# Rotary halves exchanged by transfers, and four stick-breaking steps placed ahead of the last value unit

## The reference

```python
def partial_rope(x, cos, sin):            # ROPE_DIM = 16 of 64 features of a head
    xr = x[..., :ROPE_DIM].astype(jnp.float32)
    x1, x2 = xr[..., :ROPE_DIM // 2], xr[..., ROPE_DIM // 2:]
    rot = jnp.concatenate([x1 * cos - x2 * sin, x2 * cos + x1 * sin], axis=-1)
    return jnp.concatenate([rot.astype(x.dtype), x[..., ROPE_DIM:]], axis=-1)
...
        z = jnp.einsum("bhtd,bhsd->bhts", qb, kb) * scale
        log_not = jnp.where(causal, jax.nn.log_sigmoid(-z), 0.0)
        tail = lax.cumsum(log_not, axis=3, reverse=True) - log_not
        log_a = jax.nn.log_sigmoid(z) + tail
        a = jnp.where(causal, jnp.exp(log_a), 0.0)
        outs.append(jnp.einsum("bhts,bhsd->bhtd", a, vb))
```

## Time and profile before

| | us |
|---|---|
| median of 3 runs | 2310.27 |
| profiled execution | 2309.9 |
| its span | 2307.8 |
| mean granted TensorE clock | 0.986 of full |

### The profile page before, as it was taken

The page is one execution under the profiler, slowest core; times in us unless marked ns, Lnnn a source line. Parts: engine busy times, 40 slices in busy tenths (PEclk is TensorE's granted clock), DMA queues, the critical chain, the costliest instruction groups (busy, mean ns, idle before and its releaser), DMA issues.

```text
span 2307.8 us, 28179 instructions
## 1 busy us (share of the span) xinstructions
PE 2234.9 (97%) x10366; PEld 1771.7 (77%) x10366; DVE 944.0 (41%) x1289; ACT 823.8 (36%) x1362; POOL 974.6 (42%) x435
## 2 busy tenths in 40 slices
PE   8999999999998999999999999999999889999997
PEld 6888887875556788888777888888877568888886
DVE  3211346356874411234675311134552653111345
ACT  4222335324873322223532422223342654222222
POOL 4444444553003544444443454444443434544442
PEclk9999999999998999999999999999999899999999
DMA  5222232432001322323232232222222002322221
GB/s 188 91 95 105 91 111 89 127 110 74 1 1 55 110 91 91 104 97 109 73 110 73 82 118 91 101 100 91 91 91 75 17 1 92 109 100 100 91 93 70
DMA packets 29799, 202.66 MB, mean 88 GB/s; under 512 B 3360, under 2 KB 4000, under 8 KB 6048
## 3 DMA queue, kind: packets, MB, share of 16 engines
q1 hardware_dynamic: 28800, 198.55, 24.5%
q10 hardware_dynamic: 928, 3.14, 0.4%
HBM read 198.54 MB, written 2.10 MB: 87 GB/s over the span
## 4 chain that ended last, share of the span: by engine, by line
PE 69%; DVE 4%; ACT 1%; issue 1%; POOL 1%; DVEq 0%; ACTq 0%; POOLq 0%
PE PS L946 20%; PE PS L948 20%; PE PS L947 20%; PE PS L1377 1%; PE PS L1238 1%; PE PS L1197 1%; PE PS L1269 1%; DVE NMAX L1667 1%; PE PS L1361 1%; PE PS L1389 1%; DVE ACC L1434 1%; PE PS L1017 0%; POOL X L479 0%; PE PS L1220 0%; DVE TMP L1514 0%
## 5 line engine op out<-in xcount | busy, mean ns | idle before, releaser
L454 POOL TENSOR_TENSOR WL<-RAW,WH 128x1024 fp32r<-128x1024 f32 x368 | 908.5, 2473 | 1234.4 <-ACT WH L521 1234.4
L946 PE MATMUL PS<-XH,WH 128*128 128x512 f32 (+1 forms) x2200 | 865.9, 394 | 28.9 <-DVE XL L1426 19.8
L948 PE MATMUL PS<-XH,WL 128*128 128x512 f32 (+1 forms) x2200 | 853.2, 388 | 0.0
L947 PE MATMUL PS<-XL,WH 128*128 128x512 f32 (+1 forms) x2200 | 852.8, 388 | 0.0
L521 ACT ACTIVATE WH<-RAW 128x1024 fp32r<-128x1024 f32 x368 | 388.1, 1059 | 1255.4 <-PE PS L948 1211.2
L946 PEld LDWEIGHTS PS<-XH,WH 128*128 128x128 f32 x2200 | 415.4, 189 | 125.1 <-issue 27.6
L947 PEld LDWEIGHTS PS<-XL,WH 128*128 128x128 f32 x2200 | 415.7, 189 | 86.6 <-issue 4.1
L948 PEld LDWEIGHTS PS<-XH,WL 128*128 128x128 f32 x2200 | 415.3, 189 | 84.8
L946 PE MATMUL PS<-HH,WH 128*128 128x512 f32 x672 | 261.4, 389 | 0.0
L947 PE MATMUL PS<-HL,WH 128*128 128x512 f32 x672 | 261.4, 389 | 0.0
L948 PE MATMUL PS<-HH,WL 128*128 128x512 f32 x672 | 261.4, 389 | 0.0
(11 more groups left out here) (194 smaller groups left out, 1558.2 us busy)
## 6 DMA issues: line engine op xcount, KB each, us to landing
RAW<-wstream SPq DMA_DIRECT2D x183, 1024.0 KB, 4.8
X<-xT SPq DMA_DIRECT2D x4, 512.0 KB, 9.0
WORK<-memT ACTq DMA_DIRECT2D x2, 1024.0 KB, 5.4
outT<-WORK SPq DMA_DIRECT2D x8, 256.0 KB, 2.1
RAW<-wstream SPq DMA_DIRECT2D x2, 512.0 KB, 6.3
PB<-WORK ACTq DMA_DIRECT2D x8, 127.8 KB, 2.3
CST<-consts SPq DMA_DIRECT2D x1, 912.0 KB, 10.6
WORK<-constsb SPq DMA_DIRECT2D x1, 256.0 KB, 12.4
```

Source lines behind the costliest of these rows:

```text
L454: pool.tensor_tensor(WL[:, s, :, :].rearrange("p a b -> p (a b)"), RAW[:, s, :], WH[:, s, :, :].rearrange("p a b -> p (a b)").bitcast(F), ...
L946: pe.matmul(o, wh, xh, start=start, stop=False)
L947: pe.matmul(o, wh, xl, start=False, stop=False)
L948: return pe.matmul(o, wl, xh, start=False, stop=stop)
```

## The change

Three things, the third in support of the second.

First, PERM and the matmul with it go. ScalarE, after it has rounded the next weights in a rotary job, waits for the take of that same job and issues four transfers of 8 partitions x 512 values within SBUF, from SQ to LT, which exchange the two halves of each rotary group; the other rows of LT are set to zero once at the start. The sign is in SIN. `rope` waits for the four transfers and reads LT where it read PSUM. TensorE's first attention scores wait for the takes of proj1 where `flip` did.

Second, `SB_AHEAD = 4`: steps 0 to 3 of stick-breaking are issued by TensorE before unit sv 5, and by VectorE and ScalarE before their wait for that unit. The last value units use banks 2, 3, 6, 7, two of them are transposed into their own banks, and the transposes of sv 5 go behind tails 0 and 1 and pair 4/5. The last kv unit releases the chunks of XH one by one (`XH_USERS` gains "kv").

Third, GpSimd splits units 2 and 3 of outB after the low parts of steps 0 to 7, not before them.

```diff
+def flip_bank(x):
+    return x["bank"] if x["kind"] == "sv" and x["j"] >= 4 else 4 + x["f"] % 2
...
-            split_units(first, U0["outB"] + RING)
-            low_softplus()
+            split_units(first, U0["outB"] + 2)
+            low_softplus(0, 8)
+            split_units(U0["outB"] + 2, U0["outB"] + RING)
+            low_softplus(8, len(SBSTEPS))
...
+            def rotate(x):
+                act.wait_ge(taken, x["t"] + 1)
+                for a in (0, DH):
+                    for b in (0, 8):
+                        act.dma_start(LT[a + b:a + b + 8, x["c"] % 2, :],
+                                      SQ[a + 8 - b:a + 16 - b, x["f"] % 2, :]).then_inc(rotated[x["c"] % 2], 16)
...
+                    if part == "kv" and n == len(jobs) - 1:
+                        turn(jobs[n - 2])
+                        for t in range(SB_AHEAD):
+                            sb_exp_ln(t)
                     unit(x["u"])
...
+                    if x["kind"] in ROTARY:
+                        rotate(x)
                     if x["kind"] == "vs":
                         round_b(0)
                     if x["kind"] == "ks" or (x["kind"], x["j"]) == ("nq", 1):
                         raw_hidden()
...
-                if x["kind"] in ROTARY:
-                    mm = pe.matmul(PS[:, 4 + f % 2, :], PERM, SQ[:, f % 2, :], start=True, stop=True)
...
+                        if part == "kv" and i == len(jobs) - 1:
+                            pe.wait_ge(taken, jobs[i - 2]["t"] + 1)
+                            for t in range(0, SB_AHEAD, 2):
+                                sb_pair(t)
                         features(x["u"], x["bank"], stage, first=x["n"] == 0,
...
+            for t in range(SB_AHEAD, n + LAG_V, 2):
+                if SB_AHEAD < t < n:
+                    sb_pair(t)
                 if 0 <= t - LAG_T < n:
                     sb_tail(t - LAG_T)
                     sb_tail(t + 1 - LAG_T)
+                if t == SB_AHEAD:
+                    sb_pair(t)
+                    flip(JOBS["kv"][-1])
+                if t == LAG_V:
+                    pe.wait_ge(turned, FLIPS[max(FLIPS)]["c"])
...
-                dve.wait_ge(flipped, f + 1)
-                chain(dve.tensor_tensor(TMP[:, 1, :], SIN, PS[:, 4 + f % 2, :], ALU.mult))
+                dve.wait_ge(rotated[x["c"] % 2], 64 * ((x["c"] + 1) // 2))
+                chain(dve.tensor_tensor(TMP[:, 1, :], SIN, LT[:, x["c"] % 2, :], ALU.mult))
...
+                    if last and part == "kv":
+                        for t in range(SB_AHEAD):
+                            sb_step(t)
...
+            chain(dve.memset(LT[:, :, :], 0.0))
```

More of the change, by code:

```diff
@@ L106, in bank_of @@
         return dict(slot=slot, bank=n % 4, free=t - 3 if n >= 4 else 0, after=False)
+    if part == "kv" and slot >= 16:
+        return dict(slot=slot, bank=slot - (14 if slot < 18 else 12), free=0, after=True)
     if slot >= 18:
@@ L142 @@
 FLIPS = {x["f"]: x for v in JOBS.values() for x in v if "f" in x}
+for _f, _x in FLIPS.items():
+    _x["clear"] = max([FLIPS[g]["c"] for g in range(_f % 2, _f, 2) if FLIPS[g]["kind"] in TURNED], default=0)
 XN = {n: i for i, n in enumerate(
@@ L232 @@
 LAG_T = 4
+SB_AHEAD = 4
 LAG_V = 6
@@ L354, in program @@
         flipped = sem("flipped")
+        rotated = [sem(f"rotated{i}") for i in range(2)]
         turned = sem("turned")
@@ L811, in project @@
                     round_unit(x["u"] + RING)
-                    if n >= 2 and jobs[n - 2]["kind"] in TURNED:
+                    if n >= 2 and jobs[n - 2]["kind"] in TURNED and not (part == "kv" and n == len(jobs) - 1):
                         turn(jobs[n - 2])
@@ L923, in sb_weights @@
                 act.activation(ASLOT[t % 4][:, 0:w], PS[:, t % SBANKS, 0:w], ACT.Exp).then_inc(sb_a, 1)
-            for t in range(n + LAG_T):
+            for t in range(SB_AHEAD, n + LAG_T):
                 if t >= LAG_T:
@@ L1126, in hidden_turned, with sb_scores, sb_strict, sb_tail @@
                 mm.then_inc(hid_turned, 1)
+            def sb_scores(t):
+                h, j = SBSTEPS[t]
+                if t == SB_AHEAD:
+                    pe.wait_ge(turned, FLIPS[max(FLIPS) - 2]["c"])
+                if t >= SBANKS:
+                    pe.wait_ge(sb_a, (t | 1) - SBANKS + 1)
+                r = slice(DH * (h % 2), DH * (h % 2) + DH)
+                pe.matmul(PS[:, t % SBANKS, 0:S - j * P], W[r, 8 + h // 2, j * P:(j + 1) * P],
+                          Q[r, h // 2, j * P:S], start=True, stop=False, skip_group_check=True)
+            def sb_strict(t):
+                pe.matmul(PS[:, t % SBANKS, 0:P], IDB, CSB[:, B_STRICT:B_STRICT + P], start=False, stop=False,
+                          skip_group_check=True).then_inc(sb_qk, 1)
+            def sb_tail(t):
+                h, j = SBSTEPS[t]
+                w = S - j * P
+                pe.wait_ge(sb_lo, t + 1)
+                bank = PS[:, t % SBANKS, :]
+                for n in range(NT - j):
+                    col, width, m = n * P, w - n * P, SUMS[:, 1 if n == 0 else 0, :]
+                    for part in (XH, XL):
+                        mm = pe.matmul(bank[:, col:w], m, part[:, (t - 2 * n) % 8, sb_cols(t - 2 * n, width)], start=False,
+                                       stop=n == NT - j - 1 and part is XL, skip_group_check=True)
+                mm.then_inc(sb_tri, 1)
+            def sb_values(t):
+                h, j = SBSTEPS[t]
+                c = h // 2
+                w = S - j * P
+                pe.wait_ge(sb_a, t + 1)
+                if h % 2 == 0 and j == NT - 1 and c >= 2:
+                    pe.wait_ge(sb_o, c - 1)
+                r = slice(DH * (h % 2), DH * (h % 2) + DH)
+                pe.matmul(PS[r, 6 + c % 2, j * P:S], V_SB[:, j, h * DH:(h + 1) * DH], ASLOT[t % 4][:, 0:w],
+                          start=j == NT - 1, stop=j == 0, skip_group_check=True).then_inc(sb_pv, 1)
+            def sb_pair(t):
+                sb_scores(t)
+                sb_scores(t + 1)
+                sb_strict(t)
+                sb_strict(t + 1)
             def project(part, stage, norm=None):
@@ L1154, in project @@
                         ssq(norm, 7)
-                    if i >= 1 and "f" in jobs[i - 1]:
+                    if i >= 1 and jobs[i - 1]["kind"] in TURNED:
                         flip(jobs[i - 1])
@@ L1163, in project @@
                         mem_step(MEM_BESIDE[part], k)
-                if "f" in jobs[-1]:
+                if jobs[-1]["kind"] in TURNED and part != "kv":
                     flip(jobs[-1])
@@ L1170, in scores @@
                     pe.wait_ge(roped, 10)
+                    pe.wait_ge(taken, TAKEN["proj1"] - 1)
+                if part == "mix1" and y["s"] == 2:
+                    pe.wait_ge(taken, TAKEN["proj1"])
                 if y["p"] == 4 * 4:
@@ L1350, in _ @@
             project("kv", "kv")
-            pe.wait_ge(taken, TAKEN["kv"])
-            pe.wait_ge(turned, FLIPS[max(FLIPS)]["c"])
+            pe.wait_ge(sums_ready, 1)
             n = len(SBSTEPS)
[L1356 to L1376, removed]
-                        mm = pe.matmul(bank[:, col:w], m, part[:, (t - 2 * n) % 8, sb_cols(t - 2 * n, width)], start=False,
-                                       stop=n == NT - j - 1 and part is XL, skip_group_check=True)
-                mm.then_inc(sb_tri, 1)
```

150 lines of the change are left out of this document (66 added, 84 removed).

## The result

The changed kernel took 2324.18 us (median of 5 runs, 2321.47 to 2326.82), against 2311.05 us for the kernel before on the same chip: ratio 1.006, 95% interval 1.0048 to 1.0073. One of the five runs of the kernel before took 6142.08 us, for a reason that nothing here shows, and the ratio leaves it out. Forecast were 2299.3 us and a range from 2294.5 to 2308. The profiled execution has a span of 2322.3 us, 14.5 us more than before.

The account below looks back on a forecast made before the run. The prediction took TensorE, busy 97% of the span, as the bound. Its terms, - 10.2 + 0.3 + 0.7 - 2.3 + 0.5 = - 11.0 us, gave 2299.3 us, range 2294.5 to 2308.

Parts of the forecast that it names:

- Part 1: In proj1, rotary swap matmuls leave PE's unbroken run: 12 x 0.85 = 10.2 us saved.
- Part 2: In proj1, ACT's transfers and L1556 reading LT replace the swap: small lag, 0.3 us wait ahead of w1v 0.
- the one called the weakest: On ACT's queue in rotary jobs, each 8-row transfer within SBUF was taken to cost 0.33 to 0.4 us to issue.
- The second step: In dk 0 to dk 3, DVE's lag was to grow by 0.05 us a job at 0.33 us an issue.
- Rival B: In proj1, 0.6 us issues or 6.2 us landings make PE stand 9 us twice: + 7.0, 2317 us; chance 0.12.
- Part 3: At the start of attention, L1556 waits for POOL's split and L1557 follows: first maxima + 0.7 us.
- Part 4: Around the last value unit, four steps ahead: pair 6/7 - 2.3 us, POOL's later outB splits + 0.5 us.
- Rival C: In the 512-wide scores, PE's granted clock changes: 2295.0 us (chance 0.10) or 2302.2 us (chance 0.08).
- the two of the loop: In proj1's rotary jobs: issues at 0.33 to 0.4 us, and lag growing 0.05 us a job at 0.33 us.

Follow-up runs that it names:

- the run with late ropes: The changed kernel, but VectorE ropes a job behind the next take also where a small w1 unit stands between; 2297.33 us, ratio 0.9956.

## Why the prediction was wrong

**Part 1, right.** The price of the swaps is best read in the run with late ropes, where PE waits only 0.2 us. From dk 0's take to nq 3's, in DVE's timelines, first before, then with late ropes:

```profile
453.74 0.69 DVE L1631 TENSOR_TENSOR SQ<-RSTD,PS 128x512 f32<-128x512 f32 x1 [5.24 <-PE PS L948]
...
547.92 0.69 DVE L1628 SCALAR_TENSOR_TENSOR SQ<-PS,RSTD 128x512 f32<-128x512 f32 x1 [2.71 <-PE PS L948]
```
```profile
453.26 0.69 DVE L1717 TENSOR_TENSOR SQ<-RSTD,PS 128x512 f32<-128x512 f32 x1 [5.25 <-PE PS L970]
...
537.21 0.69 DVE L1714 SCALAR_TENSOR_TENSOR SQ<-PS,RSTD 128x512 f32<-128x512 f32 x1 [1.11 <-PE PS L970]
```

94.18 less 83.95 is 10.2 us. That is net of the wait ahead of w1v 0, forecast at 0.3 us and measured there at 0.2, so the 12 swaps were 10.4 us (in the changed kernel itself that wait is gone, the stand before it having covered it).

**Part 2, wrong, in two steps of it.** The first is the one called the weakest: an issue at 0.33 to 0.4 us. It is 0.63. L819, of the same kind and engine, was the row to go by, and the reasons for setting it aside (odd row length, more rows) were guesses: 8 and 16 rows cost the same. The Trainium skill, "DMA: Bandwidth & Descriptors", on issuing engines that are not separate queues, calls the time to initiate a transfer "usually small relative to the DMA itself". For four small transfers in a row it isn't, by this trace: the issues take 2.6 us, and the last lands 2.7 us after its own began (481.41) or 2.0 us (in the dq run).

The second step would have taken most of the gain by itself: with four issues at 0.32 us the stretch from dk 0's take to the first maxima gained 2.5 us and not 9.2. The forecast let the lag grow by 0.05 us a job at 0.33 us, because it kept ACT's first rounding and POOL's first split at their places in PE's time and let only the second of each move with the take. But ACT's wait for `taken` stands ahead of both, so a take that is late enough moves both roundings, the two splits behind them, and the rope that must wait for the splits. From the rows above, closed, the period is 0.7 (take) + 4d (issues) + 0.1 + 1.1 (first rounding) + 5.2 (two splits) + 0.5 (rest of the rope) = 7.6 + 4d: 10.1 us at d = 0.63 (measured 10.2). With two issues of 0.63 it gives 8.9 (measured 8.9), with two of 0.60, 8.8 (measured 8.8), and with four of 0.32, 8.9 (measured 9.0 in every second job and 6.7 in the others). What the forecast called a lag of tenths tips into this regime as soon as both roundings are caught.

Size of the loss: the lag against the run with late ropes (whose timeline lies 0.5 us earlier) is 4.7 us after the first job already: its take stands at 465.80, there at 460.56. There the last transfer, issued about 457.6, landed at 462.66, 5.1 us later, beside a weight load issued at 457.61:

```profile
462.66 2.50 DVE L1591 TENSOR_TENSOR TMP<-CST,LT 128x512 f32<-128x512 f32 x1 [7.47 <-DMA LT<-SQ]
```

In the kernel with two transfers the second of that job was issued at 456.17 and landed at 458.19, 2.0 us later, and its load was issued only at 458.05. Each of the next jobs adds 3.3 us, the 10.2 of the ring less PE's 6.9. The Trainium skill, "DMA: Bandwidth & Descriptors", on queues, rings and completion order, has each DMA engine turn from queue to queue packet by packet; the forecast took from it that a load would not hold up a small transfer. The row of 5.1 us speaks against that, as the 6.2 us of the earlier trace rows did.

**Rival B was the case.** Its mechanism, its place (`hidden_turned`, twice) and its deciding point (0.6 us, or a landing beside a load) all came. It was too small by 7 us: its stands of 9 us were 11.4 and 11.3, PE stood 1.5 and 0.8 us for POOL's splits besides, and the half clock that it left unpriced took 4.1. These are 11.1 us more; about 4 came back behind proj1, where 5.7 us were regained and the forecast had 1.8. Its chance of 0.12 rested on the choice of 0.33 to 0.4; with L819 as the likeliest it would have been the forecast.

**Part 3, right.** From nq 3's take to the first maxima, 547.92 to 554.29, were 6.4 us; after, 7.1:

```profile
567.37 0.69 DVE L1713 SCALAR_TENSOR_TENSOR SQ<-PS,RSTD 128x512 f32<-128x512 f32 x1 [3.55 <-PE PS L970]
...
574.46 2.09 DVE L1752 TENSOR_REDUCE NMAX<-PS 128x2 f32<-128x1024 f32 x2
```

**Part 4, right within its reading.** The last value unit of the kernel after ends for ACT at 1808.57 (L529), pair 6/7 follows at 1812.85: 4.3 us instead of 8.5, forecast 4.8 (ACT's row first, then PE's and POOL's). Less the 1.5 us that now stand in front, the gain is 2.7 us (2.3). POOL's two splits cost more than the 0.5 us said:

```profile
1808.57 1.06 ACT L529 ACTIVATE WH<-RAW 128x1024 fp32r<-128x1024 f32 x1 [2.56 <-PE PS L970]
...
1812.85 2.08 PE L1155 MATMUL PS<-WORK 64*128 64x512 f32 x4 [1.99 <-ACT PB L945]
...
1822.32 4.73 POOL L460 TENSOR_TENSOR WL<-RAW,WH 128x1024 fp32r<-128x1024 f32 x2
...
1827.51 0.33 PE L1171 MATMUL PS<-XH,SUMS 128*128 128x128 f32 x1 [1.11 <-POOL XL L495]
...
1829.44 1.13 PE L1155 MATMUL PS<-WORK 64*128 64x512 f32 x4
1844.00 1.13 PE L1155 MATMUL PS<-WORK 64*128 64x512 f32 x4 [0.41 <-ACT PB L945]
```

PE waited 1.1 us for the first low part behind them. Rival C, the clock, may have played in as well: from pair to pair of the 512-wide scores it took 16.6 and 14.6 us here against 16.0 and 17.5 before. Which of the stretches is slow moves from run to run, so I give no number for it. The part as a whole gained 3.0 us (0.7 to 5.3), in the kernel that has it alone.

Summed, parts 1, 3 and 4 gave the forecast's size: the kernel with the loop open has all of the change's parts and comes to 2297.3 and 2297.7 us, ratios of 0.9956 and 0.9953, 10 to 11 us below the kernel before, where the forecast had 11.0. The wrong terms were the two of the loop. That the closed order of take, transfers, rope and next take is the cause is shown by opening it. How much of the ring's 10.2 us is due to each link is read from the traces and their sum, not shown by an edit: not tried were a loop without the lock (POOL's splits could not be taken out of DVE's way with everything else in place), and the transfers issued by another engine than ACT, which would have left the roundings out of the ring.

## What to carry to other kernels

When a transfer takes the place of a matmul, write down the ring of waits that it closes (take, issue, landing, user, next take) with every instruction queued behind the new wait on the issuing engine, and add up that ring as if nothing else set its pace. If the sum is above the period of the bound engine, the lag grows from job to job and shows where a copy of the same engine is wanted. Let the take go first and the consumer of the transfer one step later: here that one change of order turned + 0.6% into - 0.45%. For a price that the trace doesn't show, take the row of the same kind on the same engine as the likeliest, even if its shape is odd: here it said 0.53 to 0.63 us, and 0.63 was measured.

## What the runs showed of the hardware

A transfer within SBUF takes ACT's queue 0.63 us to issue with 8 rows and 0.60 us with 16, one of 8 rows to memory 0.32 us, on the same queue. Two in a row land 2.0 us after the last issue began (463.03 to 465.05 in the kernel with two transfers); four land after 2.7 us in the dk run and after 2.0 in the dq run (538.0 to 540.02), and once, beside a weight load, after 5.1 us. L1591, with two operands in SBUF, takes 0.68 us where no split of POOL runs beside it and up to 2.89 us beside one; L1556, with one operand in PSUM, never passed 0.71. This fits the exclusive lock that the Trainium skill, "SBUF — State Buffer", on who interferes with whom, states for a VectorE instruction with two SBUF inputs and a GpSimd instruction that reads SBUF. Alone, it put off the start of attention by 0.7 us. After two stands of 11 us PE came back at a granted clock of 0.50 and ran so for 5 and for 4 us.
